# RWKV-7 mixer inside a two-block model on one Trainium2 core: both halves' triangular inverses side by side, waits by true operands, second-half preparation inside the first half's state chain

## The reference

```python
def step(S, inp):
    r_t, d_t, k_t, v_t, kk_t, a_t = inp
    sa = jnp.einsum('bhij,bhj->bhi', S, -kk_t)
    S = S * d_t[:, :, None, :] + sa[..., None] * (kk_t * a_t)[:, :, None, :] + v_t[..., None] * k_t[:, :, None, :]
    return S, jnp.einsum('bhij,bhj->bhi', S, r_t)
```

## Time and profile before

| | us |
|---|---|
| median of 3 timed runs | 1478.42 |
| the three runs | 1479.66, 1478.42, 1471.74 |
| profiled execution, own time | 1478.96 |
| its span | 1477.0 |
| PE busy in the span | 1370.3 (93%) |
| DVE, ACT, POOL busy | 571.0, 617.6, 832.9 |

### The profile page before, as it was taken

One profiled execution on the slowest core, in us unless ns is written; L12 is line 12 of the kernel. 1 busy time (PEld: TensorE's weight loads), 2 busy tenths in 40 slices (PEclk: granted clock), 3 DMA queues, 4 the chain that ended last, 5 costly groups with the idle time before them and its releaser, 6 DMA issues.

```text
span 1477.0 us, 26519 instructions
## 1 busy us (share of the span) xinstructions
PE 1370.3 (93%) x11138; PEld 1282.7 (87%) x11138; DVE 571.0 (39%) x1241; ACT 617.6 (42%) x921; POOL 832.9 (56%) x419
## 2 busy tenths in 40 slices
PE   6999798787999999989999999999999977999998
PEld 5997355576999999989999999989999957999997
DVE  4545867442254565331333301232223324333301
ACT  3441152112455554444544433544545415544431
POOL 5863420002558779544687876845666505687781
PEclk9998798986989999989999999999999997999998
DMA  7945898600345555334455555443635394455540
GB/s 218 200 128 198 299 383 286 229 1 0 115 140 175 189 169 185 117 113 150 157 179 193 171 178 171 130 129 91 181 99 173 115 349 147 149 182 179 178 157 29
DMA packets 246323, 244.96 MB, mean 166 GB/s; under 512 B 25652, under 2 KB 215230, under 8 KB 246206
## 3 DMA queue, kind: packets, MB, share of 16 engines
q1 hardware_dynamic: 245715, 243.10, 51.3%
q10 hardware_dynamic: 491, 0.17, 0.1%
HBM read 242.20 MB, written 1.05 MB: 165 GB/s over the span
## 4 chain that ended last, share of the span: by engine, by line
PE 83%; DVE 6%; issue 2%; ACT 2%; DMA 2%; POOL 0%; DVEq 0%; SPq 0%; ACTq 0%
PE banks L516 82%; DVE arena L1475 2%; DMA ring<-in_attn_w_o_dram 1%; DMA ring<-in_ada_w_dram 1%; ACT arena L2147 1%; DVE masks L1479 1%; DVE banks L1482 0%; DVE ring_lo L1475 0%; PE banks L526 0%; DVE arena L1482 0%; DVE arena L1488 0%; PE banks L797 0%; DVE arena L1479 0%; ACT hn_hi L2147 0%; DVE arena L1485 0%
## 5 line engine op out<-in xcount | busy, mean ns | idle before, releaser
L1426 POOL TENSOR_TENSOR ring_lo<-ring,ring_hi 128x2048 fp32r<-128x2048 f32 (+1 forms) x176 | 718.6, 4093 | 529.5 <-ACT ring_hi L2147 529.2
L516 PE MATMUL banks<-hn_hi,ring_lo 128*128 128x256 f32 x1888 | 537.0, 289 | 0.0
L516 PE MATMUL banks<-hn_hi,ring_hi 128*128 128x256 f32 x1696 | 481.8, 289 | 7.6 <-ACT hn_hi L2147 7.6
L516 PE MATMUL banks<-hn_lo,ring_hi 128*128 128x256 f32 x1696 | 439.2, 283 | 0.0
L516 PEld LDWEIGHTS banks<-hn_hi,ring_lo 128*128 128x128 f32 x1888 | 374.6, 198 | 0.0
L2147 ACT ACTIVATE ring_hi<-ring 128x2048 fp32r<-128x2048 f32 (+1 forms) x176 | 299.4, 1703 | 154.0 <-PE banks L516 130.7
L516 PEld LDWEIGHTS banks<-hn_hi,ring_hi 128*128 128x128 f32 x1696 | 333.8, 197 | 9.5 <-issue 9.4
L516 PEld LDWEIGHTS banks<-hn_lo,ring_hi 128*128 128x128 f32 x1696 | 307.8, 192 | 0.1
L2147 ACT ACTIVATE arena<-banks 128x256 f32<-128x256 f32 (+5 forms) x227 | 89.4, 412 | 363.0 <-PE banks L516 313.0
L516 PEld LDWEIGHTS banks<-arena 128*128 128x128 f32 (+4 forms) x1342 | 135.2, 193 | 88.1 <-issue 65.0
L516 PE MATMUL banks<-arena 128*64 128x128 f32 (+9 forms) x1342 | 165.4, 321 | 46.9 <-issue 17.2
(11 more groups left out here) (221 smaller groups left out, 1699.7 us busy)
## 6 DMA issues: line engine op xcount, KB each, us to landing
ring<-in_ada_w_dram SPq DMA_DIRECT2D x48, 1024.0 KB, 9.0
ring<-in_ffn_w_up_dram SPq DMA_DIRECT2D x44, 1024.0 KB, 5.2
ring<-in_w_up_dram SPq DMA_DIRECT2D x22, 1024.0 KB, 5.2
ring<-in_ffn_w_down_dram SPq DMA_DIRECT2D x16, 1024.0 KB, 5.1
ring<-in_w_kv_dram SPq DMA_DIRECT2D x15, 1024.0 KB, 5.4
ring<-in_w_kv_dram SPq DMA_DIRECT2D x18, 512.0 KB, 3.9
ring<-in_attn_w_q_dram SPq DMA_DIRECT2D x18, 512.0 KB, 3.9
ring<-in_w_in_dram SPq DMA_DIRECT2D x8, 1024.0 KB, 12.1
```

The lines of the kernel that those rows point to most:

```text
L516: return nc.tensor.matmul(o, l, r, start=start, stop=stop, **k)
L1426: led.emit(g.tensor_tensor(low, raw, high.bitcast(F32), ALU.subtract), sem("lo_ready"))
```

## The change

- Every tile of a half gets a second copy for the other half (`TM`, `KEEP`, `tok4`, `AM`, `AU` are indexed by `s`). The new ones lie where the first inputs and parts of `hn` and `hn_hi` were.
- The first grams are N and L of both halves. PE waits for the four `L8M` masks (`tri_first`) and starts the inverses. Each of the eleven steps now makes four tiles, two per half, and waits only for the tiles it reads (`INV_NEEDS`).
- The `L16M` and `L32M` masks are no longer taken from PSUM: ACT copies `L` to `TM[s][3]`, and DVE makes both from there after the N2 copies (`tri_low`).
- The other grams and the tokens of the first half, and two of the four `ada` left, lie between inverse steps; the other two `ada` come before `mv` and after the blocks of the first half.
- Between `st` 1 and `outputs(0)` of the first half stand the second half's tokens, its three remaining grams and its `mv`.
- ACT waits for T32 of the second half before the first weight chunk too.

The core of the diff:

```diff
+        INV_NEEDS = {"L2": (), "N2": (), "L4": ("L2", "N2"), "Y1": ("L2",), "T8": ("L4", "Y1"), "T8t": ("T8",),
+                     "Ya": ("T8",), "T16": ("T8t", "Ya"), "T16t": ("T16",), "Yb": ("T16",), "T32": ("T16t", "Yb")}
...
-            pe.wait_ge(sem("gram_in"), 1)
-            for s in range(2):
...
-                            copied((INV[k - 1][0], s, p))
+                        if name in ("Ya", "Yb"):
+                            pe.wait_ge(sem("tri_low"), 4)
+                        for needed in INV_NEEDS[name]:
+                            copied((needed, s, p))
...
+            pe.wait_ge(sem("gram_in"), 1)
+            for s in range(2):
+                gram("N", s)
+                gram("L", s)
+            pe.wait_ge(sem("tri_first"), 4)
+            for s in range(2):
+                for p in range(2):
+                    copied(("N", s, p))
+            for name, lw, rw, _add, _dst in INV:
+                inverse_step(name, lw, rw)
+                if name == "Y1":
+                    tokens_out(0, (0, 1))
+                elif name == "Ya":
+                    tokens_out(0, (2, 3))
+                elif name == "Yb":
+                    gram("MT", 0)
+                elif name in ("T8", "T16"):
+                    ada()
+            gram("Rb", 0)
+            gram("Rk", 0)
+            ada()
+            masked_values(0)
+            solved(0)
+            blocks(0)
+            ada()
+            receptance(0)
+            state(1)
+            tokens_out(1, range(4))
+            state(2)
+            gram("MT", 1)
+            gram("Rb", 1)
+            state(3)
+            gram("Rk", 1)
+            masked_values(1)
+            outputs(0)
+            solved(1)
+            blocks(1)
+            receptance(1)
+            for q in (4, 5, 6):
+                state(q)
+            outputs(1)
...
-                    tt(TM[1][:, p], three(b), over3(L8M), MUL)
-                    tt(TM[2][:, p], three(b), over3(L16M), MUL)
-                    tt(TM[3][:, p], three(b), over3(L32M), MUL, *freed(("L", s, p)))
-                settle()
+                    tt(TM[s][1][:, p], three(b), over3(L8M), MUL, sem("tri_first"))
...
+                if name == "N2":
+                    for s in range(2):
+                        for p in range(2):
+                            dve.wait_ge(*freed(("L", s, p)))
+                            tt(TM[s][2][:, p], TM[s][3][:, p], over3(L16M), MUL)
+                    settle()
+                    for s in range(2):
+                        for p in range(2):
+                            tt(TM[s][3][:, p], TM[s][3][:, p], over3(L32M), MUL, sem("tri_low"))
...
+            masked((("MT", 0, U32S), ("Rb", 1, U32I), ("Rk", 2, U32I)), 0)
+            for k in range(3, 8):
+                low_part(k - 3, hn_lo[:, k, :], hn[:, k, :], hn_hi[:, k, :])
...
+            for q in (1, 2, 3):
+                state(q)
+            masked((("MT", 0, U32S), ("Rb", 1, U32I), ("Rk", 2, U32I)), 1)
+            masked_values(1)
...
+                for p in range(2):
+                    act_.wait_ge(sem("tri_first"), 2 * s + p + 1)
+                    b = take(("L", s, p))
+                    af(TM[s][3][:, p], shaped(b[:, 0:384], 3, P), ACT.Identity, *freed(("L", s, p)))
...
+            solved(0)
+            tokens_out(1, range(4))
+            outputs(0)
+            solved(1)
+            reach(("rt", 1))
+            outputs(1)
```

More of the change, by code:

```diff
@@ L200, in two_block_kernel @@
         W = [at(M0 + 768 * i, 3, T) for i in range(12)]
[L201 to L205, removed]
+        TM = [[at(M0 + 768 * i, 2, 3, P) for i in range(6)] + [at(M0 + 15360 + 768 * i, 2, 3, P) for i in range(3)],
+              [at(o, 2, 3, P) for o in (2816, 3584, 4352, 5664, 6432, M0 + 17664, M0 + 18432)] +
+              [place("hn_a", HN, F32, 2, 3, P), place("hn_b", HN + KT * T, F32, 2, 3, P)]]
+        KEEP = [[at(M0 + 12288 + 768 * i, 2, 3, P) for i in range(4)],
+                [TM[0][4], TM[0][5], TM[1][7], at(768, 2, 3, P)]]
+        tok4 = [at(M0 + 9216, 4, 3, P), at(5664, 4, 3, P)]
+        AM = [at(M0 + 10752, 3, 2, P), place("am_1", HN + KT * T, F32, 3, 2, P)]
+        AU = [at(M0 + 11520, 3, 2, P), at(1536, 3, 2, P)]
         EB, HB = at(M0, 4, 3, P), at(M0 + 1536, 4, 3, P)
@@ L1861, in _ @@
-                if s == 0:
-                    for k in range(3, 8):
-                        low_part(k - 3, hn_lo[:, k, :], hn[:, k, :], hn_hi[:, k, :])
+                        tt(KEEP[s][k][:, p], three(b), over3(m), MUL, *freed((name, s, p)))
+            for name, _l, _r, add, to in INV:
+                for s in range(2):
+                    for p in range(1 if add is None else 2):
+                        b = take((name, s, p))
+                        if add is None:
+                            copy(tmat(s, to)[:, p], three(b), *freed((name, s, p)))
+                        else:
+                            tt(tmat(s, to)[:, p], three(b), tmat(s, add)[:, p], ADD, *freed((name, s, p)))
+                if name == "N2":
+                    for s in range(2):
+                        for p in range(2):
+                            dve.wait_ge(*freed(("L", s, p)))
+                            tt(TM[s][2][:, p], TM[s][3][:, p], over3(L16M), MUL)
+                    settle()
+                    for s in range(2):
+                        for p in range(2):
+                            tt(TM[s][3][:, p], TM[s][3][:, p], over3(L32M), MUL, sem("tri_low"))
@@ L1868, in _, with blocks @@
+            def blocks(s):
                 for r in range(4):
@@ L1880, in _, with receptance, state @@
                         tt(EB[:, r], b, over3(ident[:, :]), ADD, *freed(("E", s, r)))
+            def receptance(s):
                 b = take(("rt", s))
+                cut = slice(s * P, s * P + P)
                 tt(W[9][:, :, cut], three(b), W[9][:, :, cut], ADD, *freed(("rt", s)))
                 settle()
-                for r in range(4):
-                    q = 4 * s + r
-                    if 0 < q < 7:
-                        b = three(take(("st", q)))
-                        for c in range(3):
-                            stt(ST[:, q, c, :], b[:, c, :], Pend[:, c, q:q + 1], HB[:, r, c, :], MUL, ADD,
-                                *(freed(("st", q)) if c == 2 else (None, None)))
+            def state(q):
+                b = three(take(("st", q)))
+                for c in range(3):
+                    stt(ST[:, q, c, :], b[:, c, :], Pend[:, c, q:q + 1], HB[:, q % 4, c, :], MUL, ADD,
+                        *(freed(("st", q)) if c == 2 else (None, None)))
+            masked_values(0)
+            solved(0)
+            blocks(0)
+            receptance(0)
+            for q in (1, 2, 3):
[3 more added lines that the diff above has]
+            solved(1)
+            blocks(1)
+            receptance(1)
+            for q in (4, 5, 6):
+                state(q)
             for s in range(2):
```

137 lines of the change are left out of this document (69 added, 68 removed).

## The result

| | median us | runs | ratio to before, 95% interval |
|---|---|---|---|
| before | 1479.04 | 4 | |
| the change | 1457.94 | 4 | 0.9849 [0.9820, 0.9879] |
| the change, measured again later | 1461.80 | 6 | 0.9862 [0.9834, 0.9889] |

That is 19 to 22 us less, by medians or by ratios, where 14.0 were forecast.

The account below looks back on a forecast made before the run. PE, busy 93% of the span, was taken as the bound. Its new list summed to 95.5 us against 111.19, 15.7 less; minus 1.7 for a dip, 14.0 off 1478.96 gave about 1464.5 us, range 1461 to 1469.

Parts of the forecast that it names:

- 1 start to L2: From the first transposes to the first inverse product: six transposes, first gram, then DVE's eight masks end last; 5.6 us.
- 2 inverses: Both halves' inverses up to T32: nine product steps at 3.2 us, transposes, tokens, a gram, two `ada`; 38.0 us.
- 3 to end of `au`: From T32 to the end of the first half's `au`, with DVE ending last before `au`; from 43.6 to 51.0 us.
- 4 to `st` 2: First half's blocks and first states: DVE sets `st` 2's start at 61.4 us; fourth `ada` and four token groups are free.
- 5 to end of second `au`: First half's `st` 2 to second half's `au`, grams covering DVE's work on a state; ends at 73.7 us.
- 6 second half: From the second half's `au` to the end of the second `ol`: nothing moved, same clock as before, 21.8 us.
- The clock behind the second chain: Clock after the second half's state chain, taken as before: 0.50 from 344.10 to 368.60 us in the old profile.
- the long half-rate stretch is shortened too: Rival: the half rate from 344.10 to 368.60 us shortens, some 7 to 9 us on top, 1456; chance 0.08.
- The subtraction of 1.7 for one dip: One middle-size half-rate dip assumed between the first transposes and the second half's `au`, lowering the gain from 15.7 to 14.0.
- The slower rival: Rival: the dense inverse products run at half rate, 32 us becoming 64, a loss of 16, 1495 us; chance 0.06.
- stretch of 95 to 99 us: Sign of being right: first three transposes to the end of the second `ol` takes 95 to 99 us.
- signs of being wrong: PE waiting over 1 us at T8, clock under 0.9 from L2 to T32, projection gap, or `slot_landed` wait for an `ada`.

Follow-up runs that it names:

- run with true waits: Kernel before, each inverse step waiting for the tiles it reads instead of the step before it; 1474.33 us, ratio 0.9961.
- fill experiments: Products of constants put into PE's waits: kernel before, ahead of inverses and states, 1468.73 us; changed kernel, ahead of the second half's states only, 1451.26 us.
- repeats: Unchanged kernels run again for a second trace: the changed kernel 1461.80 us, the kernel before a single time of 1482.44 us.
- version with `ada` in the chain: Changed kernel with two `ada` moved from the inverses to between states 4 and 5 of the second half; 1448.79 us, ratio 0.9776.
- fill in before: Kernel before with products of constants ahead of both inverses and the states, nothing moved; 1468.73 us, ratio 0.9917.

## Why the prediction was too small

Its parts against the two traces of the change:

| us | forecast | 1st trace | 2nd trace |
|---|---|---|---|
| 1 start to L2 | 5.6 | 5.65 | 5.65 |
| 2 inverses | 38.0 | 35.01 | 35.01 |
| 3 to end of `au` | 7.4 | 8.41 | 8.41 |
| 4 to `st` 2 | 10.4 | 10.43 | 10.43 |
| 5 to end of second `au` | 12.3 | 11.77 | 11.77 |
| 6 second half | 21.8 | 19.84 | 21.80 |
| tail | 12.19 | 8.51 | 12.19 |

- **Part 2 is the step that failed**, by its unit cost: "24 instructions take 3.19, so 1.6, and 3.2 for both halves". A step of both halves takes 2.7 to 2.8. The 35.01 us have a dip of 1.63 in them (11.27 for 84 instructions, 9.64 without it), so without it the part was 4.6 too dear. 4.3 of this are the nine product steps, 24.5 us instead of 28.8. The 3.19 was taken from the old order, in which each step waits for the copies of the step before; the profile shows that as busy. The run with true waits showed 2.94 in the old order, and 0.25 us at each step's border is 4.5 us over nine steps of two halves. With this part priced right the forecast gain would have been 18.6, already beyond the 17 at which its range ended. That DVE's eight masks cost PE nothing was right: the profile shows no wait of PE in this part. They took 3.96 us from SBUF, 0.5 each as assumed.
- **Part 3** was 1.0 too cheap. I let PE's grams run on beside DVE; but the gram `Rb` needs a bank that the mask of `MT` has to empty (by the order in which banks are given out, seven while the `ada` sum is open), and that mask stands behind four additions of T32 and begins at 287.84. The wait of 1.21 is that.
- **Parts 1, 4 and 5** came out within 0.1, 0.1 and 0.5 (the addends of part 5 give 73.5 and not the 73.7 of the prediction, so 0.2 of the 0.5 is a slip). `st` 2 started 9.8 us after the blocks, and the fourth `ada` and the tokens were free there. PE did wait 0.74 for a bank between the tokens, inside the same wait. The two grams behind `st` 2 covered DVE's work on that state.
- **The clock behind the second chain** I carried over as a constant and gave a change of it 0.08. The fill experiments show that the half rate follows the wait of 4.33 us, which the change keeps, and the repeats show that its end differs from execution to execution. In the first trace its early end gave 5.6 us, in the second nothing. So the rival "the long half-rate stretch is shortened too" is neither true nor false of this kernel but of each of its executions.
- **The subtraction of 1.7 for one dip** was right in size (1.63, at the start of the inverses), in part by luck: three of the seven traces of the changed order and its variants with the same 1.90 us wait there have it, the other four don't. It was then hidden by the too dear unit.
- The slower rival did not come: the granted clock was 0.95 over the inverses. The rule of the Trainium skill ("TensorE: Matmul & The Clock Gate", section on the HAM clock gate) that activity releases the half rate held for them. It did not hold for the end of the second chain, where five traces stayed at 0.50 for 27 us with PE busy nine tenths of the time. For the transfers there was room: nobody waited for `w_out` or `w_ple`, nor with `w_ple` issued 22 us later than in the change, in the version with `ada` in the chain.
- **The signs.** No wait between L2 and T32, `ada` between T8 and T8t without a wait, `st` 2 9.8 us behind the blocks and `w_out` from 278.65 on came as written, and none of the signs of being wrong. The stretch of 95 to 99 us did not: it was 91.1 and 93.1. So the mechanism was right, and the size of one term and the end of a half rate were not.

Together: by the means of two traces each, stretch and tail went from 124.2 to 102.4 us, 21.7 less, and the times say 19 to 22. Forecast were 14: 4.6 for part 2 and, on average, 2.8 for the end of the half rate make 21.4, less 1.0 for part 3, and 0.5 back in part 5; before's second trace, 1.6 us longer than its first, is 0.8 of the mean. The 2.8 are luck, good in one trace and absent in the other. What is not separated is how much of the clock's share (8.1 + 3.2 us by the fill in before) the change gained, and how much the shorter waits by themselves; the fill of all waits in the change's order was not run.

## What to carry to other kernels

A unit cost read from a chain of short dependent steps can have unseen waits in it, even where the profile calls the engine busy. Price the interleaved order from the distance of starts inside one step: here 24 x 0.11 is 2.7 us for a step of both halves and 24 us for nine, where 24.5 came. Where the clock falls in a wait, as TensorE's does here, the wait costs twice: fill it, if there is nothing else with work that has a place anywhere (the `ada` slices here), and put that work where the wait is longest, not where it is nearest. And look at two traces of a kernel before calling a clock stretch its property.

## What the runs showed of the hardware that I had not expected

- TensorE stayed at 0.50 (1.2 GHz) for 27 us, busy 22.82 of 25.04 us in it, in five of eight traces with a wait of 4 us ahead, and was back at 1.00 (2.4 GHz) after 7 to 10 us in the other three. With products of constants or two `ada` in the wait it had 1.00 to the end of the second `ol` in all five traces.
- The masks of a 128x384 tile cost DVE the same from SBUF as from PSUM: eight in 3.96 and eight in 3.81 us, in DVE's timeline of the change's first trace:

```profile
248.45 3.81 DVE L1536 TENSOR_TENSOR arena<-banks,masks 128x384 f32<-128x384 f32 x8 [2.81 <-PE banks L522]
...
259.41 3.96 DVE L1536 TENSOR_TENSOR arena<-arena,masks 128x384 f32<-128x384 f32 x8
```
